# Second mixer of a two-block model: scores per 64x64 block, level sums in one VectorE instruction, second tile's outputs a slot later, low weights on VectorE

## The reference

```python
def hgrn2_mixer(q, f_logit, i, og, lb, head_g):
    """S_t = diag(f_t) S_{t-1} + (1 - f_t) i_t^T ; o_t = S_t^T q_t   (per head, S in R^{A_KDIM x A_VDIM})."""
    f = lbf + (1.0 - lbf) * jax.nn.sigmoid(f_logit.astype(f32))
    k = 1.0 - f
    logf = jnp.log(f)
    qf = jax.nn.silu(q.astype(f32))
    ...
        o_inter = jnp.einsum('bhtk,bhkv->bhtv', q_ * jnp.exp(a_), S)
        decay = jnp.exp(jnp.where(causal, diff, -jnp.inf))
        scores = jnp.einsum('bhtsk,bhsk->bhts', q_[:, :, :, None, :] * decay, k_)
        o = o_inter + jnp.einsum('bhts,bhsv->bhtv', scores, v_)
```

## Time and profile before

| what | value |
|---|---|
| median of 3 runs | 3582.2 us (3581.98 to 3583.13) |
| the profiled execution's own time | 3583.97 us |
| its span, first to last instruction | 3582.2 us |
| TensorE, VectorE, ScalarE, GpSimd busy in the span | 88%, 44%, 30%, 26% |
| mean granted TensorE clock | 0.941 |
| second mixer's slots | 1764 to 2534 us of the span |
| TensorE's idle time in them behind L2467 | 73.0 us |

### The profile page before, as it was taken

The page is one execution under the profiler, slowest core; times in us unless marked ns, Lnnn a source line. Parts: engine busy times, 40 slices in busy tenths (PEclk is TensorE's granted clock), DMA queues, the critical chain, the costliest instruction groups (busy, mean ns, idle before and its releaser), DMA issues. The chain is left out here.

```text
span 3582.2 us, 51689 instructions
## 1 busy us (share of the span) xinstructions
PE 3159.8 (88%) x21264; PEld 2758.7 (77%) x21264; DVE 1566.9 (44%) x2176; ACT 1060.7 (30%) x1502; POOL 930.0 (26%) x824
## 2 busy tenths in 40 slices
PE   4996999597999999947988988888879799999997
PEld 3785888475888888837888888888877788888885
DVE  2897554232343343434364556555433123323324
ACT  3113442332221212223444444454322221121121
POOL 0221321111221222221354445445120122122121
PEclk9998999698999999978999999998989899999998
DMA  2110000212111111121111010101240111111111
GB/s 86 41 50 24 3 3 3 94 54 65 48 52 47 41 59 44 38 106 53 36 36 42 25 36 24 37 30 46 91 155 12 59 48 44 50 47 36 57 35 65
DMA packets 196731, 172.15 MB, mean 48 GB/s; under 512 B 8381, under 2 KB 179861, under 8 KB 196309
## 3 DMA queue, kind: packets, MB, share of 16 engines
q1 hardware_dynamic: 189653, 161.26, 14.0%
q10 hardware_dynamic: 6912, 8.52, 0.7%
HBM read 148.65 MB, written 21.10 MB: 47 GB/s over the span
## 5 line engine op out<-in xcount | busy, mean ns | idle before, releaser
L1674 POOL TENSOR_TENSOR ffn_w_lo<-ffn_raw,ffn_w_hi 128x1024 fp32r<-128x1024 f32 x88 | 211.9, 2418 | 1097.0 <-ACT ffn_w_hi L1734 1097.0
L1704 PE MATMUL ffn_out<-blk_hi,ffn_w_hi 128*128 128x512 f32 (+1 forms) x1584 | 443.9, 371 | 35.5 <-POOL ffn_w_lo L1674 35.5
L1704 PE MATMUL ffn_out<-blk_lo,ffn_w_hi 128*128 128x512 f32 (+1 forms) x1584 | 441.8, 369 | 0.0
L1704 PE MATMUL ffn_out<-blk_hi,ffn_w_lo 128*128 128x512 f32 (+1 forms) x1584 | 440.6, 369 | 0.0
L2579 PE MATMUL mix_e<-in_hi,mix_w_hi 128*128 128x348 f32 (+1 forms) x1056 | 365.9, 346 | 27.2 <-POOL mix_w_lo L2120 10.0
L2579 PE MATMUL mix_e<-in_lo,mix_w_hi 128*128 128x348 f32 (+1 forms) x1056 | 355.1, 336 | 0.0
L2579 PE MATMUL mix_e<-in_hi,mix_w_lo 128*128 128x348 f32 (+1 forms) x1056 | 354.7, 336 | 0.0
L1704 PEld LDWEIGHTS ffn_out<-blk_hi,ffn_w_hi 128*128 128x128 f32 x1584 | 290.8, 190 | 79.2 <-POOL ffn_w_lo L1674 19.6
L1704 PEld LDWEIGHTS ffn_out<-blk_lo,ffn_w_hi 128*128 128x128 f32 x1584 | 290.1, 190 | 43.1
L1704 PEld LDWEIGHTS ffn_out<-blk_hi,ffn_w_lo 128*128 128x128 f32 x1584 | 289.0, 190 | 43.5
L1734 ACT ACTIVATE ffn_w_hi<-ffn_raw 128x1024 fp32r<-128x1024 f32 x88 | 90.9, 1054 | 740.8 <-PE ffn_out L1704 728.8
(11 more groups left out here) (327 smaller groups left out, 5575.8 us busy)
## 6 DMA issues: line engine op xcount, KB each, us to landing
ffn_raw<-ffn_up SPq DMA_DIRECT2D x44, 512.0 KB, 3.9
mix_raw<-w_in SPq DMA_DIRECT2D x44, 512.0 KB, 3.8
ffn_raw<-w_up SPq DMA_DIRECT2D x44, 512.0 KB, 3.9
ffn_d_raw<-ffn_down SPq DMA_DIRECT2D x11, 1024.0 KB, 5.9
ffn_d_raw<-w_down SPq DMA_DIRECT2D x11, 1024.0 KB, 6.0
proj_w_raw<-w_in_first SPq DMA_DIRECT2D x20, 512.0 KB, 4.1
branch_gates<-proj SPq DMA_DIRECT2D x16, 520.0 KB, 4.9
wout_raw<-w_out SPq DMA_DIRECT2D x16, 512.0 KB, 4.0
```

The costliest lines, as they stand in the source:

```text
L1674: G.by(nc.gpsimd.tensor_tensor(w_lo[:, i % 2], raw[:, i % 2], w_hi[:, i % 2], ALU.subtract), f"lo{i}")
L1704: mm = nc.tensor.matmul(o, a[:, i % 2, k, :], b[:, k, first:first + n], start=k == 0 and part == 0, stop=k == KD - 1 and part == 2)
```

## The change

- `scores` makes the products only where they can be needed: for the diagonal and levels 0 to 5 the two 64x64 blocks on a tile's diagonal, each with 64 columns of the array (the upper one in the lower columns, the other in the upper), and for level 6 one product of 128x64. All eight results are in one PSUM bank of 8 x 64 columns. Level 0 needs no distances: its product is k by q times f, which VectorE makes with one instruction in `forget`.
- GpSimd's `halve` and VectorE's `add` are replaced by one `tensor_reduce` over seven levels on VectorE, right behind the mask. The eighth result, the upper right block, is left apart.
- `outputs` has two products with the upper 64 keys, the state's product, then the update, and last a product with the lower 64 keys, which waits for the state's product (`upper_ready`). Those of a unit's second tile stand in the next slot, behind its first dense piece.
- From block 10 on the low weights are made by VectorE; GpSimd has distances alone. The last keys' distances are made inside ScalarE's exp (scale -1, the end of the tile as bias).
- The pool `e` has three banks; `la`, `qa` are three deep, `o` and `out` two. The spreads of a pair of heads stand one slot later, one by one. Three slots instead of six have a fourth dense piece, so the tail has six pieces; the sums stand behind four of them.

```diff
-LONGER = (5, 10, 15, 20, 25, 30)
+LONGER = (5, 13, 21)
+BANKS = 3
+DISTANCES = 6
...
-            def halve(u, i):
-                g, n = number(u, i), size(i)
-                pool.wait_ge(masked, g + 1)
-                lv = 4 if i < FULL2 else 1
-                m = mk[g % 2][0:n]
-                tt(m[:, 0:lv, 0:n], m[:, 0:lv, 0:n], m[:, 4:4 + lv, 0:n], ALU.add).then_inc(halved, 1)
...
+            for u in range(1, slots):
+                for l in range(1, LEVELS2):
+                    distances(u, l)
...
             def last_level(u):
-                act.wait_ge(dlast_ready, u + 1)
-                activation(kl[:, 0, 0:UNIT], kl[:, 0, 0:UNIT], ACT.Exp).then_inc(elast_ready, 1)
+                if u:
+                    await_piece(act, "kt", u - 1)
+                for i in range(2):
+                    a = sf[:, (u // UNITS) % 2, cols_of(u)][:, i * P:(i + 1) * P]
+                    done = activation(kl[:, 0, i * P:(i + 1) * P], a, ACT.Exp, scale=-1.0, bias=a[:, P - 1:P])
+                done.then_inc(elast_ready, 1)
...
+                dve.wait_ge(floor_ready, u + 1)
+                vec.tensor_tensor(z[u % 2][:, 0, 0:width(u)], q[:, h % 2, cols_of(u)], f, ALU.mult).then_inc(z_ready, 1)
...
-                src = sc[g % 2][:].rearrange("p a (l b) -> p (a l) b", b=P)
-                m = masks[:].rearrange("p (l b) -> p l b", b=P)
-                vec.tensor_tensor(mk[g % 2][0:n, 0:lv, 0:n], src[0:n, 0:lv, 0:n], m[0:n, 0:lv, 0:n], ALU.mult).then_inc(
+                src = sc[0:n, g % 2, :].rearrange("p (l b) -> p l b", b=C1)
+                vec.tensor_tensor(mk[g % 2][0:n, 0:lv, 0:m], src[:, 0:lv, 0:m], masks[0:n, 0:lv, 0:m], ALU.mult).then_inc(
                     masked, 1)
-
-            def add(u, i):
-                g, n = number(u, i), size(i)
-                dve.wait_ge(halved, g + 1)
-                m = mk[g % 2][0:n]
-                vec.tensor_tensor(m[:, 0:2, 0:n], m[:, 0:2, 0:n], m[:, 2:4, 0:n], ALU.add).then_inc(added, 1)
+                dve.wait_ge(masked, g + 1)
+                lv = min(lv, 7)
+                vec.tensor_reduce(own[0:n, g % 2, 0:m], mk[g % 2][0:n, 0:lv, 0:m].rearrange("p l b -> p b l"), AX.X,
+                                  ALU.add).then_inc(added, 1)
...
+            def weight_lo_by(p):
+                n = p // 3 + 1
+                if p % 3 == 0 and FIRST_LO <= n < CHUNKS2:
+                    dve.wait_ge(hi_ready, n + 1)
+                    dve.wait_ge(lo_ready, n)
+                    vec.tensor_tensor(w_lo[:, n % 2], raw[:], w_hi[:, n % 2], ALU.subtract).then_inc(lo_ready, 1)
...
-                for l in range(8 if i < FULL2 else 5):
-                    lhs = k[:, u % 2, cs] if l == 0 else z[u % 2][:, l - 1, cs]
-                    rhs = q[:, head, i * P:i * P + n] if l == 0 else z[u % 2][:, l - 1, cs]
-                    last = mm(sc[g % 2][0:n, l // 4, (l % 4) * P:(l % 4) * P + n], lhs, rhs, start=True, stop=True)
+                parts = [slice(0, C1), slice(C1, P)] if i < FULL2 else [slice(0, TAIL2)]
+                for l in range(7 if i < FULL2 else 5):
+                    lhs = keys_ if l < 2 else z[u % 2][:, l - 1, cs]
+                    rhs = queries_ if l == 0 else z[u % 2][:, l - 1, cs]
+                    for own_ in parts:
+                        last = mm(sc[own_, g % 2, l * C1:l * C1 + own_.stop - own_.start], lhs[:, own_], rhs[:, own_],
+                                  start=True, stop=True, skip_group_check=True)
+                if i < FULL2:
+                    zz = z[u % 2][:, LEVELS2 - 1, cs]
+                    last = mm(sc[:, g % 2, 7 * C1:8 * C1], zz, zz[:, C1:P], start=True, stop=True,
+                              skip_group_check=True)
...
-                for l in range(2):
-                    last = mm(out[hp, cs], vt[0:n, i, hp], mk[g % 2][0:n, l, 0:n], start=first and l == 0,
-                              stop=l == 1 and i == 0, skip_group_check=True)
+                mm(out[hp, u % 2, c:c + C1], vt[upper, i, hp], own[upper, g % 2, :], start=first, stop=False,
+                   skip_group_check=True)
+                last = mm(out[hp, u % 2, c + C1:c + P], vt[upper, i, hp], mk[g % 2][upper, 7, :], start=False, stop=False,
+                          skip_group_check=True)
...
+                last.then_inc(upper_ready, 1)
+                update(u, i)
+                pe.wait_ge(upper_ready, h * FULL2 + i + 1)
+                mm(out[hp, u % 2, c + C1:c + P], vt[lower_, i, hp], own[lower_, g % 2, :], start=False, stop=True,
+                   skip_group_check=True).then_inc(out_ready, 1)
```

More of the change, by code:

```diff
@@ L2526, in _ @@
             for u in range(slots):
-                more, tiles = u + 1 < slots, tiles_of(u)
+                more, dense, tiles = u + 1 < slots, pieces_of_slot(u), tiles_of(u)
+                spreading = u % 8 == 1 and u > 8
+                for i in before(u)[2:]:
+                    mask(u - 1, i)
                 if more:
                     forget(u + 1)
-                mask(u, tiles[0])
-                if more:
                     scan(u + 1)
                     queries(u + 1)
-                    level(u + 1, 0)
@@ L2535, in _ @@
-                add(u, tiles[0])
+                for p in pieces_of_slot(u - 1)[2:] if u else []:
+                    weight_lo_by(p)
                 if more:
                     level(u + 1, 1)
+                if spreading:
+                    finish(u // 8 - 1, 0)
+                if u:
+                    state(u - 1, before(u)[1])
+                if more:
+                    level(u + 1, 2)
+                mask(u, tiles[0])
+                weight_lo_by(dense[0])
+                if more:
+                    level(u + 1, 3)
+                    level(u + 1, 4)
@@ L2545, in _ @@
-                for i in tiles[2:]:
-                    mask(u, i)
-                add(u, tiles[1])
-                state(u, tiles[1])
-                for i in tiles[2:]:
-                    add(u, i)
-                if u and u % 8 == 0:
-                    finish(u // 8 - 1)
-                if more:
-                    for l in range(5, LEVELS2):
-                        level(u + 1, l)
-                    last_keys(u + 1)
+            mask(slots - 1, FULL2)
+            for p in pieces_of_slot(slots - 1)[2:]:
+                weight_lo_by(p)
@@ L2684, in _ @@
                 outputs(u, tiles[0])
-                update(u, tiles[0])
+                if spreading:
+                    spread(u // 8 - 1, 2)
                 dense(pieces[2])
```

315 lines of the change are left out of this document (162 added, 153 removed).

## The result

The changed kernel takes **3427.8 us** (median of 4 runs, 3426.1 to 3428.5), the kernel before 3582.7 (3582.0 to 3586.7) beside it: ratio 0.9565, 95% interval 0.9548 to 0.9581. That is 155 us less; forecast were 127 less (3455), with a range of 3415 to 3520. The profiled execution took 3427.2 us, its span is 3425.4.

The account below looks back on a forecast made before the run. TensorE was taken as the bound, though not a full one, with 73.0 us waiting for the second sum over levels. Terms -78 - 40 - 12 + 6 - 4 = -128 us from 3584.0 gave 3456, as median about 3455; range 3415 to 3520.

Parts of the forecast that it names:

- What bounds the kernel: Second mixer's 32 slots: TensorE bounds, but not fully; its output products wait 73.0 us for the second sum over levels.
- Term 1: TensorE's waits in the slots: 73.0 us for the sum and 5.1 for the last level go, -78 us.
- Term 2: Clock in the second mixer: falls behind waits, so three quarters of 55 us come back, -40 us (bounds 0 and -62).
- Term 3: TensorE's own work per tile: 2.81 us against 3.00, with 7 changes of form instead of 2, -12 us over 64 tiles.
- Term 4: New wait of the lower half's output product for the state product: about 0.1 us, 64 times, +6 us.
- Low weights, reduce, mask: VectorE's steps in the slots: low weights 1.2 us each, reduce 0.6, mask 0.68; hidden, with VectorE's slot at 12.5 us.
- Term 5: The mixer's tail: four dense pieces ahead of the last head's sums of squares remove waiting and half clock, -4 us.
- A: Rival in the slots: the next unit's chain sets the slot, so the gain is only 83 us, 3500 us; chance 0.20.
- B: Rival in the scores: the two halves' products do not run side by side, +54 us, 3509 us; chance 0.12.
- C: Rival in all 32 slots: the finer pattern of short records holds the clock down, slower, 3600 us; chance 0.04.
- D: Rival: the waits move rather than go, no measurable change, 3582 us; chance 0.04.

Follow-up runs that it names:

- pool_lo: The changed kernel with the low weights from block 10 on back on GpSimd, between its distances: 3421.9 us, ratio 0.9565.
- late_start: The changed kernel with VectorE's mask and sum of the first tile back ahead of the next unit's scan and queries: 3501.3 us, ratio 0.9770.
- full_rows: The changed kernel with all output products over 128 keys, against copies of v whose other half is 0: 3404.2 us, ratio 0.9501.
- corner64: The changed kernel with the last score product (level 6) only 64x64, its other quarter set to 0 once: 3412.2 us, ratio 0.9525.
- before_reduce: The kernel before with GpSimd's level sum and VectorE's second sum replaced by one VectorE reduce right behind the mask: 3524.8 us, ratio 0.9837.

## Why the prediction was right, step by step

- **What bounds the kernel.** Right. The mixer alone changed, and the time came from the wait for the sum. The chain as read from the earlier trace rows was tested in parts: without GpSimd's stage the wait falls to 10.7 us in the kernel before. One link was read too simply. The level products ahead of VectorE's second sum are not only in its way, they are held up themselves:

```profile
2083.20 1.56 DVE L2445 TENSOR_TENSOR mix_work<-mix_work 128x128 f32<-128x128 f32 x1
2084.68 1.38 DVE L2445 TENSOR_TENSOR mix_work<-mix_q,mix_work 128x128 f32<-128x128 f32 x1
```

  The first ends at 2084.76, just behind GpSimd's low weights (2084.61), the second at 2086.06, just behind its level sum (2085.91). In the slots of the kernel before, 48 level products took over 0.7 us. All of them started inside one of these two GpSimd instructions (20 the low weights, 28 the level sum) and ended 0.15 to 0.16 us after it; together they took 80.6 us, where 48 at 0.28 are 13. Eight more, which started within 0.04 us of a level sum's start, took their 0.28 to 0.29. The changed kernel has none. pool_lo has 27 again (54.4 us) and loses no time by them, since VectorE has room there.
- **Term 1, waits, -78.** Measured -92.8 of idle time. The 78.1 went whole. The difference is mostly what I left as it was, the dense pieces behind ScalarE (9.2 in the earlier trace rows, and rows of 3.7, 2.9 and 1.0 that are not shown, the 2.9 behind VectorE): "a third bank can only shorten them" was too timid. The third bank is not what did it, since the change with two banks shows none of the `mix_iv` waits either. And I took 5.1 us for the next unit's first steps standing ahead of the masks, where late_start shows that this order carries 73 us: the sum was right there because nothing went wrong, not because it was priced.
- **Term 2, clock, -40.** Measured -48.3, mean 0.99 in the slots (said: 0.97 or more). The step "three quarters of 55" was too small because nearly all of the waiting went. Idle time and clock loss go together from kernel to kernel: 114.5 and 55.4, 96.1 and 45.8, 88.0 and 39.9, 77.1 and 33.3, 72.6 and 31.0, 21.7 and 7.1. Among the kernels with 20 to 28 us of idle time (clock 4.3 to 8.6) the order is not so strict. The granted clock falls behind waits of TensorE, and a us of waiting removed gave back about 0.5 more. The bound of -62 held.
- **Term 3, work, -12.** Measured -18.5. 2.68 us a tile, and 2.77 with the change of form ahead of the scores, against 2.81; 64 times 3.00 less 2.77 is 15, and the other 4 us are traced to no row. The price of a change, 0.13, fits: the tile's time without changes was priced at 1.90, and if that holds, (2.77 - 1.90) / 7 is 0.12. The Trainium skill (TensorEngine Tiling (Array Packing), Key Properties) has it that a change of tiling mode drains the array; the traces agree in that each change costs time, and full_rows and corner64 won time by having fewer of them.
- **Term 4, new wait, +6.** Measured about 0. From the update's start to the lower half's product it is 0.37 us (2022.90 to 2023.27), which is the update's 0.25 and one change of form. The 0.1 was most likely a double count: the change of form takes at least as long as the latency that the wait is for.
- **Low weights, reduce, mask.** The subtraction takes 1.29 us (said 1.2), the mask 0.69 (0.68), both hidden. The reduce takes **0.95** us, not 0.6: I took it from the middle of the bounds 0.28 to 1.21 by its element count, as if it cost what a product does. It moved no time, since a dense piece covers it. VectorE's slot is 11.1 us and not 12.5: the levels' products take 0.34 us on average where I had left them at the 0.55 of the earlier trace rows. The traces show why: a product of 128x128 with no GpSimd instruction beside it takes 0.28 to 0.29 us in both kernels (179 of 370 before, 186 of 324 after); one with GpSimd beside it for at least half of its time takes 0.69 on average before and 0.44 after.
- **Term 5, tail, -4.** Right, about -3. In the changed kernel the sums of squares start at 2380.09 without a wait (1.58 before) and take 1.95 us instead of 3.01, and the dense piece behind them loses about 0.5 us less. These are parts of the idle time and clock above.
- **Rivals.** A did not happen. late_start, at its place, ends at 3501 beside the 3500 given to A, but by waits for the state and not for level products, so A's price was not tested. B did not happen; forced, it costs 0.64 us a tile where I had priced 0.84, since a record of 64 columns alone takes 0.053 us (28 in 1.60 less one change of form), not 0.06. C fell: the clock rose with the finer pattern. D fell in the changed kernel; before_reduce shows a piece of it, since there some of the waits moved to the banks.

Sum: -92.8 - 48.3 - 18.5 is -159.6 for the mixer; forecast -128. (The span fell by 156.8, since the mixer's first matmul came 3.2 us later in the changed kernel's profiled execution.) Each of the three was too small, none in the wrong place. The 32 us between them are 15 of waits, 8 of clock, 6 of work, and 2 net of terms 4 and 5, which lie inside the measured numbers.

## What to carry to other kernels

When the bound engine waits for a chain over two other engines, count what stands ahead of each link in its engine's queue: the crossing and the place in the queue cost more here than the arithmetic. Put the first steps of the next unit ahead of any step that waits for the bound engine; that order alone was worth 73 us in the changed kernel. In the old one, where steps of ScalarE moved with it, the waits for banks grew and it lost 20. A long instruction on GpSimd can hold VectorE as well as its own queue. On TensorE count changes of form, not only columns: at about 0.12 us each, they made it worth 23 us to multiply with zeros and stay in one form.

## What the hardware showed beyond expectation

- Two products in different column halves overlap when issued in turns (28 records in 0.96 us) and hardly at all in two groups (1.60 us).
- In the kernel before, 48 of the 56 level products on VectorE that started inside GpSimd's low weights or level sum ended only 0.15 to 0.16 us after that instruction: up to 2.46 us instead of 0.28.
- A reduction over strided levels costs 0.95 us for 448 elements and 1.99 for 1024, where a product of 512 elements takes 0.69: about 2 ns an element read against 1.3.
- TensorE's wait for its own product, with one instruction issued between (0.73 us from start to start), showed no cost of its own where the array changed form anyway.
- TensorE's waiting came with 0.43 to 0.48 us of clock loss for each us of it, in all five kernels of the table with more than 70 us of idle time.
